# Five affine passes over the first token chunk move from the second projections' weight splits to the first output projection

## The chip, the core and the metric

The kernel runs on one core of one Trainium2 chip. A core has five instruction streams that run side by side and meet at semaphores: PE (TensorE, matrix products), DVE (VectorE), ACT (ScalarE), POOL (GpSimd), and SP (SyncE), which here only issues DMAs. The metric is the device time of one launch in microseconds (us). The kernel before took 1267.05 us, the median of three runs (1266.28 to 1267.63).

## The reference, cut to what matters

One decoder layer over 1024 tokens of width 1024. The part that the change touches is the first LayerNorm's result, which is needed twice: transposed, as the input of the projections, and by rows, as the residual of the first output projection.

```python
x = layer_norm(x, emb_ln_g, emb_ln_b)                 # rows: x_hat * g + b
proj = x @ w_in[l]                                    # pool channels u, queries q, latent c, indexer iq/ik/iw
pooled = causal_multiscale_pool(u_pool)               # windows 2, 4, 8, 16: one group of 128 channels each
pool_out = einsum(pooled, pool_w) * pool_scale
o_lat = dsa_sparse_attention(q_lat, c, iq, ik, iw, rel_bias)   # indexer scores, top 256, softmax
mix = concatenate([pool_out, attn_out]) @ w_o[l]      # the output projection
x = layer_norm(ALPHA * x + mix, ln1_g[l], ln1_b[l])   # the residual uses the rows x
ff = square(relu(x @ w_up[l])) @ w_down[l]
x = layer_norm(ALPHA * x + ff, ln2_g[l], ln2_b[l])
```

## The kernel before, in words

**Chunks and stages.** The tokens go in two chunks of 512, each of four blocks of 128 rows. The order on PE is: projections of chunk 0, projections of chunk 1, attention of chunk 0, output projection of chunk 0, MLP of chunk 0, then attention, output projection and MLP of chunk 1. Each stream's order is written out by hand; nothing is scheduled by a tool.

**Weights.** Every weight matrix is cut into units of 128 x 1024 numbers (512 KB). A unit passes three streams. SP loads it into one of four buffers of a ring (`wring`, `load_unit`); the load of unit n waits until unit n-4 has been split. ACT rounds it to the high part (`hi`, L1226). POOL, for most units, subtracts the two to get the low part (`lo`, which calls `split_lo`, L417). PE then forms hi x hi, hi x lo and lo x hi (L1540 to L1542). The output projection of chunk 0 has eight units, named wo(nh, u): nh is the half of the output columns, u the quarter of the inner dimension. The four of nh = 1 go to buffers of their own (`wo_hi`, `wo_lo`); the other four share the two `whi`/`wlo` buffers with everything else.

**The rows of chunk 0.** The normalized rows without gain and bias are spilled to memory early, and come back into `rows` before chunk 1's projections end. `emb_gains` on POOL then makes two passes over each of the four blocks: times the gain (L786), plus the bias (L788): eight passes, written mult0, add0, ..., mult3, add3 below. Each add raises the semaphore `emb_rows`. It is a generator: whoever calls `next` gets one pass. The gains lie in `gains`; once all four blocks are done, SP loads the gain and bias of the next LayerNorm over them (`load_gains`, L448 and L449).

**Around the pooling.** In `products(1)` PE projects q0, q1, q2, u0, u1, u2, u3 and q3 of chunk 1, and forms the four small products po0 to po3 (L1626) among and behind them. DVE makes the pooled channels in `pooling` (L584 to L604), with more and more adds from window 2 to window 16; po3 waits for the last. Meanwhile POOL splits the weights of the units ahead. The attention of chunk 0 begins behind po3: POOL prepares the head masks (L778, first wait on po3), DVE adds them to the logits (L1005).

**The output projection of chunk 0.** PE, DVE and ACT all walk the same list, `projection_steps`: first nh = 0 by u and then by block b, then nh = 1 by block and then by u. After each of the first sixteen steps one indexer dot product of chunk 1 is slipped in: PE forms it (`dot`, L1604 and L1605), ACT takes its relu (`relu_dots`, L1292), DVE adds it to the scores (`add_score`, L931). With two buffers for each, dot n waits for relu n-2, and relu n for score n-2. ACT also rounds the weights to come at set steps of the list: wo(1,1) at step (0,2,1) ahead of relu 25, wo(1,2) at (0,2,3) ahead of relu 27, wo(1,3) at (0,3,1) ahead of relu 29, the first MLP unit at (0,3,3) ahead of relu 31. `add_residual` on DVE adds the rows at u = 3 and takes the statistics; POOL turns them into 1/std (`inverse_std`, L743 and L745) behind its splits of the first two MLP units.

Of the kernel before, what the change touches and what calls it, by code (L numbers as in the profile page):

```python
# [41 lines left out]
CB = CHUNK // P  # L42
# [93 lines left out]
def layer(nc, x, emb_ln_g, emb_ln_b, rel_bias, w_in, pool_w, pool_scale, kv_norm_g, w_uk, w_uv, w_o,  # L136
# [15 lines left out]
    with ExitStack() as ctx:  # L152
# [3 lines left out]
        def sem(name):  # L156
            return ctx.enter_context(nc.semaphore(name))
# [125 lines left out]
        rows_in = sem("rows_in")  # L283
# [18 lines left out]
        emb_rows = sem("emb_rows")  # L302
# [47 lines left out]
        units = []  # L350
# [6 lines left out]
        U = {name: n for n, name in enumerate(units)}  # L357
# [54 lines left out]
        def split_lo(eng, name, sem_lo, at=None):  # L412

            n = U[name]

            eng.wait_ge(hi_ready, n + 1 if at is None else at)
            eng.tensor_tensor(parts_of(name, lo_tile(name)), parts_of(name, wring[n % 4]),  # L417
                              parts_of(name, hi_tile(name)).bitcast(F32), ALU.subtract).then_inc(sem_lo, 1)
# [11 lines left out]
        def _(sp):  # L430
            def load_unit(name):
                n = U[name]
                slot = wring[n % 4]
                if n >= 4:

                    sp.wait_ge(*LO[units[n - 4]])
                if name[0] == "wo":
                    _, c, nh, u = name
                    sp.dma_start(k_pairs(slot), wod[:, 2 * u:2 * u + 2, nh * 512:nh * 512 + 512]).then_inc(ring_in[n % 4], 16)
                elif name[0] == "ik":  # L440

                    sp.dma_start(parts_of(name, slot), wind[:, :, COL_IK:COL_IK + KEYW]).then_inc(ring_in[n % 4], 16)
                else:
                    col = {"c": COL_C, "iq": COL_IQ, "q": COL_Q, "u": COL_U}[name[0]] + (P * name[2] if name[0] != "c" else 0)
                    sp.dma_start(k_columns(slot), wind[:, :, col:col + P]).then_inc(ring_in[n % 4], 16)

            def load_gains(g, b):
                sp.dma_start(gains[:, 0, :], g.to_broadcast([P, D])).then_inc(gains_in, 16)  # L448
                sp.dma_start(gains[:, 1, :], b.to_broadcast([P, D])).then_inc(gains_in, 16)  # L449

            def load_mlp(c):

                first = U[("mlp", c, 0)]
                sem_lo, lo_base = LO[("mlp", c, 0)]

                sp.wait_ge(*LO[units[first - 1]])
                for g in range(GROUPS):
                    for j in range(GUNITS):
                        load_mlp_unit(c, g, j)
                        if c == 1:  # L460
                            if (g, j) == (0, 6):

                                sp.wait_ge(x1_rows, 2 * CB)
                                load_gains(ln2_g, ln2_b)
                            if j == 8 and g:
                                store(g - 1)
                            continue
                        if (g, j) == (0, 8):

                            sp.wait_ge(proj_full, 2 * CB)  # L470
                            sp.wait_ge(relu_ready, 48)
                            sp.dma_start(emb_rows_g[:, 0, :], emb_ln_g.rearrange("(o d) -> o d", o=1).to_broadcast([P, D])).then_inc(emb_gain_in, 16)
                            sp.dma_start(emb_rows_g[:, 1, :], emb_ln_b.rearrange("(o d) -> o d", o=1).to_broadcast([P, D])).then_inc(emb_gain_in, 16)
                        if j == 8:
                            load_stage(g)
                        if j == 4 and g:
                            store_stage(g - 1)
                if c:
                    store(CB - 1)
                    return  # L480
                store_stage(CB - 1)
# [32 lines left out]
            def load_units(names):  # L514
                for name in names:
                    load_unit(name)
# [40 lines left out]
            for b in range(CB):  # L557
                sp.dma_start(rows[:, b, :], spilld[b]).then_inc(rows_in, 16)
            load_units(units[U[("iq", 1, 3)]:U[("wo", 0, 1, 0)]])
            sp.wait_ge(emb_rows, CB)  # L560
            load_gains(ln1_g, ln1_b)
            load_units(units[U[("wo", 0, 1, 0)]:U[("mlp", 0, 0)]])
            load_mlp(0)
            load_units(units[U[("wo", 1, 0, 0)]:U[("wo", 1, 1, 0)]])

# [57 lines left out]
        def projection_steps():  # L623

            return [(0, u, b) for u in range(4) for b in range(CB)] + [(1, u, b) for b in range(CB) for u in range(4)]
# [5 lines left out]
        def dots_after(c, nh, u, b):  # L631

            return [16 + 4 * u + b] if c == 0 and nh == 0 else []

        def rows_of(c):
            return score if c else rows
# [67 lines left out]
        def _(pool):  # L704
# [58 lines left out]
            def head_masks(c):  # L763


                pool.wait_ge(g_full, EV[("po", 1, 3)])
                for m in range(32 * c, 32 * c + 32):
                    i, h = divmod(m, HEADS)
                    length = (i + 1) * P
                    near = min(NEAR, length)  # L770
                    if h == 0 and i >= 2:
                        pool.wait_ge(mask_ready, i - 1)
                    if m >= 2:

                        pool.wait_ge(masked, m - 1)
                    if h < 2 and length > NEAR:
                        pool.tensor_copy(mask[:, m % 2, 0:length - NEAR], score[:, i % CB, 0:length - NEAR])
                    pool.tensor_tensor(mask[:, m % 2, length - near:length], score[:, i % CB, length - near:length],  # L778
                                       near_bias[:, h, NEAR - near:NEAR], ALU.add).then_inc(mask_full, 1)

            def emb_gains():

                pool.wait_ge(gains_in, 32)
                for b in range(CB):
                    pool.wait_ge(rows_in, 16 * (b + 1))
                    link(pool.tensor_tensor(rows[:, b, :], rows[:, b, :], gains[:, 0, :], ALU.mult))  # L786
                    yield b
                    pool.tensor_tensor(rows[:, b, :], rows[:, b, :], gains[:, 1, :], ALU.add).then_inc(emb_rows, 1)  # L788
                    yield b
# [17 lines left out]
            def lo(*names):  # L807
                for name in names:
                    split_lo(pool, name, lo_pool)
# [24 lines left out]
            gained = emb_gains()  # L834
            for name in units[U[("iq", 1, 3)] + 3:U[("wo", 0, 0, 2)]]:
                lo(name)
                next(gained)
            head_masks(0)
            lo(*units[U[("wo", 0, 0, 2)]:U[("mlp", 0, 0)]])
            lo(("mlp", 0, 0), ("mlp", 0, 1))  # L840
            inverse_std(LN1_0)

# [29 lines left out]
        def _(dve):  # L872
# [203 lines left out]
            def add_residual(c, l):  # L1076


                dve.wait_ge(rows_in, 16 * CB * (c + 1))
                dve.wait_ge(emb_rows, CB * (c + 1))  # L1080
                for nh, u, b in projection_steps():
                    n = 8 * c + 4 * nh + b
                    if u == 3:
                        dve.wait_ge(proj_full, n + 1)
                        piece = rows_of(c)[:, b, nh * 512:nh * 512 + 512]
                        nc.vector.scalar_tensor_tensor(out=piece, in0=piece, scalar=ALPHA, in1=bank(("proj", c, nh, b))[:, :],
                                                       op0=ALU.mult, op1=ALU.add).then_inc(wo_added, 1)
                        dve.wait_ge(wo_added, n + 1)
                        nc.vector.bn_stats(stats[:, b, 6 * nh:6 * nh + 6], piece).then_inc(bn_ready, 1)
                        if nh == 1:  # L1090
                            dve.wait_ge(bn_ready, n + 1)
                            nc.vector.bn_aggr(mean_var[:, 4 * l + b, :], stats[:, b, :]).then_inc(stats_ready, 1)
                            x1_norm(c, l, b)
                            if b == CB - 2:
                                x1_lo(dve, c, 0, range(3))
                    if c and (nh, u, b) == (0, 2, CB - 1):
                        for piece in range(4):
                            split_lo(dve, ("wo", 1, 1, piece), lo_dve)
                    if c and (nh, u, b) in ((0, 3, CB - 1), (1, 0, 0)):
                        split_lo(dve, ("mlp", 1, nh), lo_dve)  # L1100
                    for d in dots_after(c, nh, u, b):
                        add_score(d)
                x1_lo(dve, c, 0, [3])
                x1_lo(dve, c, 1, range(4))
# [759 lines left out]
```

## Time and profile before

| what | value |
|---|---|
| median of the runs | 1267.05 us |
| the profiled execution's own time | 1263.58 us |
| its span | 1261.8 us |
| PE, DVE, ACT, POOL busy | 96%, 66%, 44%, 41% |
| chain that ended last | PE 84%, DVE 6%, POOL 5%, ACT 2%, issue 2%, DMA 1% |
| mean granted TensorE clock | 0.992 |

The profile is of one execution. Its busy shares are averages over stages with different limits, so a stage is read by itself, in its own stretch of the span. The chain that ended last is followed back from the last instruction, and says which engine's work or wait each microsecond hangs on. A row of a timeline shows in brackets how long the engine sat idle ahead of it and who released it. The granted clock is 1.00 where TensorE ran at 2.4 GHz and 0.50 where it ran at 1.2 GHz.

### The profile page before, as it was taken

The page shows a single profiled execution, that of the slowest core. Times are in us where ns is not written, and L with a number is a line of the kernel's source. Part 1 is how long each engine was busy: PE and PEld are TensorE (multiplying, and loading weights), DVE is VectorE, ACT ScalarE, POOL GpSimd, SP SyncE. Part 2 cuts the span into 40 slices and gives each one's busy share as a digit, 9 for nine tenths or more (in the row PEclk, how much of TensorE's full clock was granted, in tenths as well). Part 3 has the DMA queues.
Part 4 walks back from the last instruction along what each step waited for, and adds up shares of the span by engine and source line. Part 5 has one row for each costly group of instructions (what it writes and reads, how often), then busy time and mean ns, then how long its engine had stood idle before and what let it go on. Part 6 is the DMA issues. An engine that isn't in the chain of part 4 may idle for free.

```text
span 1261.8 us, 16530 instructions
## 1 busy us (share of the span) xinstructions
PE 1208.7 (96%) x5761; PEld 979.6 (78%) x5761; DVE 833.4 (66%) x1201; ACT 557.7 (44%) x943; POOL 512.5 (41%) x370
## 2 busy tenths in 40 slices
PE   5999997989999999999999999989899999999997
PEld 3776785778788778788788789978788888888886
DVE  6388989557857888888988766647534233243357
ACT  4546542775165234244243366652342442433440
POOL 2235798424435676775865752202102102103002
PEclk9999999899999999999999999999999999999999
DMA  7723431101314333243242200024132333423331
GB/s 221 250 76 106 145 100 52 66 1 34 101 34 134 100 101 117 84 133 100 84 132 90 94 1 2 1 101 134 63 100 88 105 101 95 117 84 99 116 102 66
DMA packets 126564, 117.59 MB, mean 93 GB/s; under 512 B 5741, under 2 KB 99498, under 8 KB 126506
## 3 DMA queue, kind: packets, MB, share of 16 engines
q1 hardware_dynamic: 126506, 116.81, 30.4%
q8 instruction: 37, 0.61, 0.2%
q14 instruction: 21, 0.17, 0.0%
HBM read 106.29 MB, written 10.50 MB: 93 GB/s over the span
## 4 chain that ended last, share of the span: by engine, by line
PE 84%; DVE 6%; POOL 5%; ACT 2%; issue 2%; DMA 1%; POOLq 0%; DVEq 0%; ACTq 0%
PE g_bank L1540 16%; PE g_bank L1542 16%; PE g_bank L1541 16%; PE wide L1540 9%; PE wide L1542 9%; PE wide L1541 9%; PE g_bank L1500 4%; POOL wlo L417 2%; PE wide L1645 1%; DVE win L588 1%; PE wide L1604 1%; PE wide L1605 1%; PE g_bank L1692 1%; POOL rows L805 1%; POOL rstd L745 1%
## 5 line engine op out<-in xcount | busy, mean ns | idle before, releaser
L417 POOL TENSOR_TENSOR wlo<-wring,whi 128x1024 fp32r<-128x1024 f32 (+1 forms) x94 | 229.6, 2444 | 226.0 <-ACT whi L1413 121.7
L1540 PE MATMUL g_bank<-xhi,whi 128*128 128x512 f32 (+2 forms) x768 | 300.7, 392 | 4.8 <-DVE xlo L654 3.8
L1542 PE MATMUL g_bank<-xhi,wlo 128*128 128x512 f32 (+2 forms) x768 | 296.9, 387 | 0.0
L1541 PE MATMUL g_bank<-xlo,whi 128*128 128x512 f32 (+2 forms) x768 | 296.8, 386 | 0.0
L1413 ACT ACTIVATE whi<-wring 128x1024 fp32r<-128x1024 f32 x120 | 127.1, 1059 | 355.8 <-PE wide L1542 179.8
L417 DVE TENSOR_TENSOR wlo<-wring,whi 128x1024 fp32r<-128x1024 f32 (+1 forms) x66 | 84.4, 1279 | 197.6 <-ACT whi L1413 192.7
L1540 PE MATMUL wide<-whi,hhi 128*128 128x512 f32 x480 | 190.2, 396 | 0.7 <-POOL wlo L417 0.7
L1542 PE MATMUL wide<-whi,hlo 128*128 128x512 f32 x480 | 189.6, 395 | 0.0
L1541 PE MATMUL wide<-wlo,hhi 128*128 128x512 f32 x480 | 189.6, 395 | 0.0
L1540 PEld LDWEIGHTS g_bank<-xhi,whi 128*128 128x128 f32 (+1 forms) x768 | 143.8, 187 | 39.9 <-DVE xlo L654 4.3
L1541 PEld LDWEIGHTS g_bank<-xlo,whi 128*128 128x128 f32 (+1 forms) x768 | 143.9, 187 | 33.0 <-issue 1.8
L1542 PEld LDWEIGHTS g_bank<-xhi,wlo 128*128 128x128 f32 (+1 forms) x768 | 143.8, 187 | 33.0 <-issue 0.6
L989 DVE MAX8 top<-work 128x8 f32<-128x640 f32 (+3 forms) x128 | 131.6, 1028 | 18.7 <-DVE work L992 0.2
L743 POOL TENSOR_SCALAR rstd<-mean_var 128x1 f32<-128x1 f32 x24 | 9.1, 381 | 301.5 <-DVE mean_var L884 232.9
L992 DVE MATCH_REPLACE8 work<-top,work 128x640 f32<-128x640 f32 (+3 forms) x128 | 129.2, 1010 | 0.0
L1540 PEld LDWEIGHTS wide<-whi,hhi 128*128 128x128 f32 x480 | 90.0, 187 | 24.5 <-POOL wlo L417 2.9
L1542 PEld LDWEIGHTS wide<-whi,hlo 128*128 128x128 f32 x480 | 90.0, 187 | 22.1
L1541 PEld LDWEIGHTS wide<-wlo,hhi 128*128 128x128 f32 x480 | 90.0, 187 | 21.8
L1226 ACT ACTIVATE whi<-wring 128x1024 fp32r<-128x1024 f32 (+1 forms) x40 | 41.6, 1041 | 115.7 <-PE g_bank L1542 99.5
L1005 DVE CUSTOM_DVE_ANT_0 logit<-wide,mask 128x128 f32<-128x128 f32 (+7 forms) x64 | 48.4, 756 | 53.2 <-PE g_bank L1500 44.9
L778 POOL TENSOR_TENSOR mask<-score,near_bias 128x256 f32<-128x256 f32 (+1 forms) x64 | 44.7, 701 | 74.0 <-DVE neg_max L1005 69.3
L931 DVE SCALAR_TENSOR_TENSOR score<-relu_sb,idx_w,score 128x384 f32<-128x384 f32 (+5 forms) x42 | 56.6, 1369 | 19.3 <-ACT relu_sb L1292 18.0
(215 smaller groups left out, 1993.4 us busy)
## 6 DMA issues: line engine op xcount, KB each, us to landing
wring<-in_w_up SPq DMA_DIRECT2D x64, 512.0 KB, 4.0
wring<-in_w_down SPq DMA_DIRECT2D x64, 512.0 KB, 3.7
wring<-in_w_in SPq DMA_DIRECT2D x26, 512.0 KB, 3.9
wring<-in_w_o SPq DMA_DIRECT2D x16, 512.0 KB, 4.6
rows<-in_x SPq DMA_DIRECT2D x8, 512.0 KB, 5.0
normalized_rows<-rows SPq DMA_DIRECT2D x8, 512.0 KB, 6.9
rows<-normalized_rows SPq DMA_DIRECT2D x4, 512.0 KB, 5.2
emb_stage<-normalized_rows SPq DMA_DIRECT2D x4, 512.0 KB, 4.8
```

The lines of the kernel that those rows point to most:

```text
L417: eng.tensor_tensor(parts_of(name, lo_tile(name)), parts_of(name, wring[n % 4]), parts_of(name, hi_tile(name)).bitcast(F32), ALU.subtract) ...
L778: pool.tensor_tensor(mask[:, m % 2, length - near:length], score[:, i % CB, length - near:length], near_bias[:, h, NEAR - near:NEAR], ALU. ...
L931: nc.vector.scalar_tensor_tensor(out=s, in0=relu_sb[:, n % 2, 0:length], scalar=idx_w[:, i, h:h + 1], in1=s, op0=ALU.mult, op1=ALU.add)\
L989: nc.vector.max(top8[:, 0, :], w).then_inc(topk_steps, 1)
L992: nc.vector.match_replace(w, top8[:, 0, :], w, TAKEN).then_inc(topk_steps, 1)
L1005: nc.vector.tensor_tensor_reduce(logit[:, m % 2, 0:length], wide[m % 2][:, 0:length], mask[:, m % 2, 0:length], -1.0, -TAKEN, ALU.add, ALU ...
L1226: nc.scalar.activation(parts_of(name, hi_tile(name)), parts_of(name, wring[n % 4]), ACT.Copy).then_inc(hi_ready, 1)
L1413: nc.scalar.activation(whi[(R[("mlp", c, 0)] + j) % 2][:, :], wring[(first + j + 2) % 4][:, :], ACT.Copy)\
L1500: last = nc.tensor.transpose(ps[:, n * P:n * P + rows_in_part] if rows_in_part == P else ps[:, 0:rows_in_part], part, ident[0:rows_in_part ...
L1540: nc.tensor.matmul(out_ap, w_hi, m_hi, start=first, stop=False)
L1541: nc.tensor.matmul(out_ap, w_hi, m_lo, start=False, stop=False)
L1542: return nc.tensor.matmul(out_ap, w_lo, m_hi, start=False, stop=last)
```

## The change

Three of the eight passes (mult0, add0, mult1) stay beside the weight splits of chunk 1's projections. The other five are taken behind the head masks of chunk 0: two behind the split of wo(0,2), two behind that of wo(0,3), one behind that of wo(1,0). `add_residual` waits for each block's own rows instead of for all four ahead of the first step. SP loads wo(1,0) ahead of its wait for the four blocks, and the other three units of nh = 1 still behind it.

```diff
@@ SP
             load_units(units[U[("iq", 1, 3)]:U[("wo", 0, 1, 0)]])
+            load_units(units[U[("wo", 0, 1, 0)]:U[("wo", 0, 1, 1)]])
             sp.wait_ge(emb_rows, CB)
             load_gains(ln1_g, ln1_b)
-            load_units(units[U[("wo", 0, 1, 0)]:U[("mlp", 0, 0)]])
+            load_units(units[U[("wo", 0, 1, 1)]:U[("mlp", 0, 0)]])
             load_mlp(0)
@@ POOL
             gained = emb_gains()
             for name in units[U[("iq", 1, 3)] + 3:U[("wo", 0, 0, 2)]]:
                 lo(name)
-                next(gained)
+                if name[0] == "u" and name[2] < 2 or name[0] == "q" and name[2] == 2:
+                    next(gained)
             head_masks(0)
-            lo(*units[U[("wo", 0, 0, 2)]:U[("mlp", 0, 0)]])
+            for name in units[U[("wo", 0, 0, 2)]:U[("mlp", 0, 0)]]:
+                lo(name)
+                for _ in range(2):
+                    next(gained, None)
@@ DVE, add_residual
-                dve.wait_ge(rows_in, 16 * CB * (c + 1))
-                dve.wait_ge(emb_rows, CB * (c + 1))
                 for nh, u, b in projection_steps():
                     n = 8 * c + 4 * nh + b
                     if u == 3:
+                        dve.wait_ge(rows_in, 16 * CB * (c + 1))
+                        dve.wait_ge(emb_rows, CB * c + (b + 1 if c == 0 else CB))
                         dve.wait_ge(proj_full, n + 1)
```

POOL's stream beside the projections of chunk 1, in the kernel before, from the split of the unit u2 to the first head mask (`wlo` is the low part of a weight unit):

```order
L417 TENSOR_TENSOR wlo1<-wring1,whi1 128x1024 [waits hi_ready,pool_steps]
L788 TENSOR_TENSOR rows<-rows,gains 128x1024
L417 TENSOR_TENSOR wlo0<-wring2,whi0 128x1024 [waits hi_ready]
L786 TENSOR_TENSOR rows<-rows,gains 128x1024 [waits rows_in]
L417 TENSOR_TENSOR wlo1<-wring3,whi1 128x1024 [waits hi_ready,pool_steps]
L788 TENSOR_TENSOR rows<-rows,gains 128x1024
L417 TENSOR_TENSOR wlo0<-wring0,whi0 128x1024 [waits hi_ready]
L786 TENSOR_TENSOR rows<-rows,gains 128x1024 [waits rows_in]
L417 TENSOR_TENSOR wlo1<-wring1,whi1 128x1024 [waits hi_ready,pool_steps]
L788 TENSOR_TENSOR rows<-rows,gains 128x1024
L778 TENSOR_TENSOR mask_56<-score,near_bias 128x128 [waits g_full]
```

In the changed kernel the five splits stand there alone. The five passes stand behind the last head mask of chunk 0, among the splits for the output projection (in this kernel's line numbers, L787 is the gain, L789 the bias; `wo_lo00` to `wo_lo03` belong to wo(1,0) to wo(1,3)):

```order
L417 TENSOR_TENSOR wlo0<-wring2,whi0 128x1024 [waits hi_ready]
L789 TENSOR_TENSOR rows<-rows,gains 128x1024
L787 TENSOR_TENSOR rows<-rows,gains 128x1024 [waits rows_in]
L417 TENSOR_TENSOR wlo1<-wring3,whi1 128x1024 [waits hi_ready,pool_steps]
L789 TENSOR_TENSOR rows<-rows,gains 128x1024
L787 TENSOR_TENSOR rows<-rows,gains 128x1024 [waits rows_in]
L417 TENSOR_TENSOR wo_lo00_90<-wring0,wo_hi00_82 128x1024 [waits hi_ready,pool_steps]
L789 TENSOR_TENSOR rows<-rows,gains 128x1024
L417 TENSOR_TENSOR wo_lo01_91<-wring1,wo_hi01_83 128x1024 [waits hi_ready]
L417 TENSOR_TENSOR wo_lo02_92<-wring2,wo_hi02_84 128x1024 [waits hi_ready]
L417 TENSOR_TENSOR wo_lo03_93<-wring3,wo_hi03_85 128x1024 [waits hi_ready]
```

SP's stream around the wait for the four blocks, before and with the change:

```order
-L439 DMA wring<-in_w_o 128x2x512 [waits lo_pool] x4
+L439 DMA wring<-in_w_o 128x2x512 [waits lo_pool] x5
 L448 DMA gains<-in_ln_g 128x1024 [waits emb_rows]
 L449 DMA gains<-in_ln_b 128x1024
-L439 DMA wring<-in_w_o 128x2x512 [waits lo_pool] x4
+L439 DMA wring<-in_w_o 128x2x512 [waits lo_pool] x3
 L507 DMA wring<-in_w_up 128x8x128 [waits lo_pool] x8
```

The wait on `emb_rows` stands one unit later in the stream, and what it waits for now ends in the output projection.

## Rows read from the trace of the kernel before

**Rows 1.** Page, part 4: chain that ended last, shares by engine.

```profile
PE 84%; DVE 6%; POOL 5%; ACT 2%; issue 2%; DMA 1%; POOLq 0%; DVEq 0%; ACTq 0%
```

**Rows 2.** Timeline of PE, 204 to 224 us: start, duration, line, instruction, [idle before <- releaser].

```profile
206.23 1.12 PE L1626 MATMUL g_bank<-pooledT,poolw 128*128 128x512 f32 x2 [0.65 <-DVE pooledT L604]
213.61 1.12 PE L1626 MATMUL g_bank<-pooledT,poolw 128*128 128x512 f32 x2 [0.65 <-DVE pooledT L604]
221.84 2.07 PE L1626 MATMUL g_bank<-pooledT,poolw 128*128 128x512 f32 x2 [7.10 <-DVE pooledT L604]
```

**Rows 3.** Timeline of DVE, pooling of chunk 1.

```profile
206.29 0.71 DVE L588 TENSOR_TENSOR win<-uT 128x527 f32<-128x527 f32 x1
...
214.61 2.55 DVE L588 TENSOR_TENSOR win<-win 128x526 f32<-128x526 f32 x1
217.20 2.19 DVE L593 COPY win<-uT 128x2 f32<-128x2 f32 x1
...
220.16 0.17 DVE L593 COPY win<-uT 128x4 f32<-128x4 f32 x1
...
221.09 0.69 DVE L604 SCALAR_TENSOR_TENSOR pooledT<-win,uT 128x512 f32<-128x512 f32 x1
```

**Rows 4.** Timeline of POOL, same stretch.

```profile
206.81 2.45 POOL L417 TENSOR_TENSOR wlo<-wring,whi 128x1024 fp32r<-128x1024 f32 x1 [1.18 <-ACT whi L1226]
...
214.26 2.34 POOL L417 TENSOR_TENSOR wlo<-wring,whi 128x1024 fp32r<-128x1024 f32 x1 [2.18 <-ACT whi L1226]
216.56 2.80 POOL L788 TENSOR_TENSOR rows<-rows,gains 128x1024 f32<-128x1024 f32 x1
224.00 0.87 POOL L778 TENSOR_TENSOR mask<-score,near_bias 128x128 f32<-128x128 f32 x2 [4.64 <-PE g_bank L1626]
```

**Rows 5.** Timeline of ACT, pooling of chunk 1.

```profile
206.63 0.58 ACT L1193 ACTIVATE uT<-g_bank 128x512 f32<-128x512 f32 x1
...
213.06 1.06 ACT L1226 ACTIVATE whi<-wring 128x1024 fp32r<-128x1024 f32 x1 [4.98 <-PE g_bank L1542]
```

**Rows 6.** Stretch: us, busy PE, PEld, DVE, ACT, POOL, then granted clock, DMA share, GB/s.

```profile
222.00:226.00 4.00, 3.77 (x10) 2.42 (x11) 0.60 (x4) 1.57 (x5) 1.74 (x4) 0.50 0.97 357
```

**Rows 7.** Timeline of POOL, output projection of chunk 0.

```profile
290.67 2.40 POOL L417 TENSOR_TENSOR wlo<-wring,whi 128x1024 fp32r<-128x1024 f32 x1 [21.99 <-ACT whi L1226]
299.39 2.42 POOL L417 TENSOR_TENSOR wlo<-wring,whi 128x1024 fp32r<-128x1024 f32 x1 [6.32 <-ACT whi L1226]
301.77 9.43 POOL L417 TENSOR_TENSOR wo_lo<-wring,wo_hi 128x1024 fp32r<-128x1024 f32 x3
```

**Rows 8.** Timeline of SP, issues around the gains of the next LayerNorm.

```profile
219.38 0.34 SPq L448 DMA_DIRECT2D gains<-in_ln_g  x1
...
220.25 0.43 SPq L439 DMA_DIRECT2D wring<-in_w_o  x1
```

**Rows 9.** DMA issues, 219.5 to 220.45 us, then 301 to 303 us: last number us to landing.

```profile
wring<-in_w_o SPq DMA_DIRECT2D x1, 512.0 KB, 7.5
...
wring<-in_w_o SPq DMA_DIRECT2D x1, 512.0 KB, 3.7
```

**Rows 10.** Timeline of ACT, output projection of chunk 0.

```profile
301.82 1.05 ACT L1226 ACTIVATE wo_hi<-wring 128x1024 fp32r<-128x1024 f32 x1
303.32 0.81 ACT L1292 ACTIVATE relu_sb<-wide 128x768 f32<-128x768 f32 x1 [0.44 <-PE wide L1605]
...
312.85 1.05 ACT L1226 ACTIVATE wo_hi<-wring 128x1024 fp32r<-128x1024 f32 x1
```

**Rows 11.** Timeline of PE there: dot 27, start of nh = 1, its end.

```profile
306.73 0.40 PE L1604 MATMUL wide<-key_hi,iq 128*128 128x512 f32 x1
...
316.38 0.39 PE L1540 MATMUL g_bank<-wo_hi,pool_hi 128*128 128x512 f32 x1
...
339.73 2.56 PE L1508 MATMUL wide<-ident 128*128 128x128 f32 x22
```

**Rows 12.** Timeline of DVE, last residual add of chunk 0.

```profile
342.02 0.68 DVE L1086 SCALAR_TENSOR_TENSOR rows<-rows,g_bank 128x512 f32<-128x512 f32 x1
```

## The prediction, made before the changed kernel ran

> **What bounds the kernel now.** I read the chain that ended last first: 84% of it is PE [rows 1]. So a microsecond counts where PE stands still, or where PE's next work comes later; where POOL or DVE merely get busier it costs nothing. I then looked on PE's timeline for idle time near the change. There is one big gap: PE has done po2 and stands 7.10 us until DVE has the last pooled tensor, so po3 starts only at 221.84 [rows 2]. The attention of chunk 0 hangs on it: the first head mask starts at 224.00, having waited for po3 [rows 4]. In the output projection of chunk 0, PE goes without a gap from the first step to 340.1 (the filler that follows it starts at 339.73, and I take 0.4 us for the last product's end) [rows 11]; there ACT, POOL and SP are early enough by a margin, and the change spends that margin. Those are the two places to work out.
>
> **Place 1: the pooling of chunk 1.** Beside POOL's work DVE's instructions are stretched. One and the same add takes 0.71 us when POOL is idle (it starts at 206.29, POOL's next pass starts at 206.81 and ends late) and 2.55 us when a weight split runs from 214.26 to 216.60: DVE starts at 214.61 and ends at 217.16, which is the split's end plus 0.56. A copy of 2 columns takes 2.19 beside a pass over the rows, one of 4 columns takes 0.17 alone [rows 3, 4]. So whoever comes second waits for the whole of the other's instruction. The Trainium skill ("SBUF — State Buffer", Who interferes with whom) says this of VectorE instructions with two SBUF inputs against GpSimd: an exclusive lock, not a sharing of bandwidth. By that rule, the trace agrees, but it also speaks against the change, since the score adds in the output projection read two SBUF inputs too.
>
> With the passes gone, DVE's last group (window 16) goes as follows. u3 reaches DVE at 206.63 + 0.58 = 207.21 [rows 5]. The split at 206.81 ends at 209.26 [rows 4] and holds the first copy until then. Behind it stand 4 adds at 0.71, 4 small instructions at 0.16 and the last one at 0.69 [rows 3], with about 0.04 between them: 4.4 us. The pooled tensor is there at 213.6. No other POOL pass lies in the way: the next split follows ACT's rounding, which waits for q3. q3 ends 0.65 us earlier than before, since po1's wait of 0.65 goes [rows 2] (its group ends well ahead); ACT rounds at 213.06 - 0.65 = 212.4 for 1.06 us [rows 5], and POOL splits from 213.6 to 216.0. Hence po3 starts near 213.7 instead of 221.84, and the first head mask, now behind the split, at 216.05 instead of 224.00: **7.95 us** earlier. Late next is thus POOL's split, not DVE.
>
> The clock adds a little. In the gap it falls to 0.50 and is still 0.50 from 222 to 226 while PE works [rows 6]: po3's two parts take 2.07 us where po2's take 1.12 [rows 2]. [...] What stands on the path after 224.00 are short products between longer waits; I take 0.75 us, bounds 0 and 1.5 (half of the 3 us or so of work at the low level). Place 1 gives **-8.7 us**, between -7.5 and -9.5.
>
> **Place 2: the output projection of chunk 0.** I keep the times of before here, and subtract place 1 at the end. POOL's split of wo(0,2) is at 290.67 to 293.07, followed now by add1 and mult2, which just fit ahead of the next split (299.39): even at 3.14 us each (see below) they end at 299.35 [rows 7]. From 299.39 five instructions now stand in a row: the split of wo(0,3), add2, mult3, the split of wo(1,0), add3. Alone one takes 2.40; three of them beside busy DVE score adds took 9.43, 3.14 each [rows 7]. Low end 5 x 2.40 = 12.0, high end 5 x 3.14 = 15.7. DVE has score adds in its queue for about three of the five and then runs dry (below), so 3 x 3.14 + 2 x 2.40 = 14.2: add3 ends, and `emb_rows` reaches 4, at **313.6** (311.4 to 315.1).
>
> Only then does SP leave its wait. It issues the two gain loads and wo(1,1), wo(1,2), wo(1,3). In the trace the same sequence starts at 219.38, the first unit is issued at 220.25 [rows 8] and lands 7.5 us later [rows 9]: 8.4 us from the end of the wait. The same load with nothing ahead of it lands in 3.7 [rows 9]; with the 0.9 us of issuing that is the low end, 4.6. I take 8.4, since the queue is the same: wo(1,1) is there at **322.0** (316.0 to 324). The Trainium skill ("DMA: Bandwidth & Descriptors", Anatomy of one DMA) gives some 2.0 us plus the bytes at 436 GB/s: for three loads of 512 KB an estimate of 5.6 us, by which the time would be 2.8 us shorter than I forecast. The trace shows more for the same three, so the sum goes by it.
>
> wo(1,1) is wanted early. ACT rounds it at 301.82, ahead of relu 25 [rows 10]. Its stream is in order, so ACT now stands at this rounding for 322.0 - 301.8 = 20.2 us. Queued behind it: relus 25 to 31 and all later roundings. Dot 27 needs relu 25, so PE stops where it stood at 306.73 [rows 11]. DVE runs out of scores after number 24. Nothing else can use the time: the projection steps of u = 3 stand behind dot 27 on PE.
>
> After the load (t = 322.0): rounding and relu 25 end at t + 1.8, and PE resumes. From there relus alternate with score adds, which wait behind POOL's splits: score 25 ends at t + 4.5, relu 27 at t + 5.5, score 26 at t + 8.0, relu 28 at t + 8.75, and then ACT rounds wo(1,3). Before, that was 312.85 - 301.82 = 11.0 us behind the rounding of wo(1,1); now it is 8.75, because the backlog of scores is gone: 2.3 us come back. Lateness from there: 20.2 - 2.3 = 17.9.
> The same by PE: it resumes at 323.8 instead of 306.73, 17.1 late. After 17 us of idle its clock will be at 0.50 for some 5 us, as it was after 7 us [rows 6], worth 2 to 3 us: it begins nh = 1 at t + 14.3 = 336.3 instead of 316.38, 19.9 late. But PE had some 1.9 us to spare: it ended at 340.1 while DVE, going block by block through the norm, made its last residual add at 342.02 [rows 11, 12]. 19.9 - 1.9 = 18.0. Both ways give **+18.0 us**. With the low end of the load (316.0) it is +12.0; with the high end (324) and all of the clock's price, +22.
>
> **The rest at nothing.** The per-block waits on DVE: block b's rows are ready at or ahead of 313.6, and the first step that wants them now comes past 323, so they never end last; behind such a wait would stand score adds. Without this edit DVE would have stood ahead of its first score. Loading wo(1,0) one place earlier only fills a free buffer. The next LayerNorm's gains land by 319, and are first used behind the statistics, past 340. From the MLP on all moves as one, since PE is the chain.
>
> **Sum.** 18.0 - 8.7 = **+9.3 us**. Against the profiled execution's 1263.58 that is 1272.9; the median of the runs stands 3.5 above it, and I apply the difference to the median: 1267.05 + 9.3 = **1276.4 us**.
>
> **Rivals.**
> A. A shorter stall. POOL's five instructions hardly meet DVE and the three units come in without a tail: t = 316.0, so +12.0 - 8.7 = +3.3, 1270.4. For it: a load alone lands in 3.7. Against: two 512 KB loads stand ahead of it in the same queue.
> B. A longer one. t = 324, and PE's low clock is not absorbed by the 1.9 us: +22 - 7.5 = +14.5, 1281.5. For it: no idle of 17 us is in the trace to show the recovery; against: the margin at 342.02.
> C. DVE's pooling is slow by itself, and place 1 gives nothing: +18.0, 1285. The pair of 0.71 and 2.55 us for the same instruction speaks against it.
> D. The faster side. The wait for wo(1,1) is not last: if its load came so early that place 2 costs less than 8.7 us, the kernel gains; with place 2 at nothing it takes 1267.05 - 8.7 = 1258.4. It decides from a landing at t = 312.7 in before's times. But five instructions of 2.40 us from 299.39 end at 311.4 and the load takes 4.6 at least, so it would need POOL to reach add3 earlier, or ACT to have slack of 3 us and more that I overlook.
>
> **Chances.** Forecast 0.60, A 0.17, B 0.13, C 0.04, D 0.06. A measurement of this kernel tells 0.2% (2.5 us) from no change. Slower by more: forecast, B, C and nearly all of A: 0.93. Within it: 0.03, the low edge of A. Faster: 0.04 of D. The range takes in A and most of B: 1270 to 1282.
>
> **What would show it.** Right: PE's wait ahead of po3 under 1.5 us and no low clock there; the first head mask near 216; on SP a wait for the rows' bias pass (L789) that ends in the output projection; on ACT 15 to 20 us idle ahead of a `wo_hi` rounding, put down to a DMA; PE idle some 16 us ahead of dot 27, the granted clock at 0.50 behind it. Wrong: ACT not idle there (D), the pooling's instructions still above 2 us with no split beside them (C), or `emb_rows` complete ahead of 311 in before's times. Then step "313.6" or step "8.4 us" has failed, and their rows say which.

## The result, and the profile after

The changed kernel took 1275.23 us (median of four runs, 1274.52 to 1278.06); the kernel before took 1266.91 us beside it. The ratio is 1.0070, 95% interval 1.0052 to 1.0087: about 8.3 us slower. The forecast was 9.3 us slower, 1276.4 us.

Both places are in the trace. First the pooling. This is PE's timeline of the changed kernel, 200 to 232 us; it answers to [rows 2]:

```profile
215.59 1.12 PE L1631 MATMUL g_bank<-pooledT,poolw 128*128 128x512 f32 x2 [0.69 <-DVE pooledT L605]
```

Of the three waits for pooled tensors one is left, the one ahead of po3, and it is 0.69 us instead of 7.10. DVE's timeline of the last channel group says why, beside [rows 3]:

```profile
209.26 2.00 DVE L585 COPY uT<-hist 128x16 f32<-128x16 f32 x1 [1.13 <-ACT uT L1198]
211.29 0.71 DVE L589 TENSOR_TENSOR win<-uT 128x527 f32<-128x527 f32 x1
212.03 0.15 DVE L594 COPY win<-uT 128x1 f32<-128x1 f32 x1
212.22 0.71 DVE L589 TENSOR_TENSOR win<-win 128x526 f32<-128x526 f32 x1
...
214.84 0.69 DVE L605 SCALAR_TENSOR_TENSOR pooledT<-win,uT 128x512 f32<-128x512 f32 x1
```

The add over 526 columns, 2.55 us before, takes 0.71. Only the first copy is held. POOL's timeline has the weight split that holds it, and behind the next split the first head mask (compare [rows 4]):

```profile
208.82 2.40 POOL L417 TENSOR_TENSOR wlo<-wring,whi 128x1024 fp32r<-128x1024 f32 x1 [4.06 <-ACT whi L1231]
215.27 2.47 POOL L417 TENSOR_TENSOR wlo<-wring,whi 128x1024 fp32r<-128x1024 f32 x1 [4.05 <-ACT whi L1231]
217.70 0.86 POOL L779 TENSOR_TENSOR mask<-score,near_bias 128x128 f32<-128x128 f32 x2
```

Clock times of two profiled executions must not be subtracted as they stand. This one is 2.0 us late when the pooling begins, a point that the change doesn't reach (DVE's first copy starts at 191.60, before at 189.59); its first projections ran partly at the lower clock (granted clock 0.91 from 20 to 40 us, 1.00 in before). So I measure from that copy. The first mask came 34.41 us behind it before, and 26.10 us now: 8.3 us are won.

Now the output projection. These are POOL's seven instructions from the split of wo(0,3) on, as in [rows 7]:

```profile
293.39 2.44 POOL L417 TENSOR_TENSOR wlo<-wring,whi 128x1024 fp32r<-128x1024 f32 x1 [0.64 <-ACT whi L1231]
295.79 3.26 POOL L789 TENSOR_TENSOR rows<-rows,gains 128x1024 f32<-128x1024 f32 x1
299.01 3.33 POOL L787 TENSOR_TENSOR rows<-rows,gains 128x1024 f32<-128x1024 f32 x1
302.42 2.81 POOL L417 TENSOR_TENSOR wo_lo<-wring,wo_hi 128x1024 fp32r<-128x1024 f32 x1
305.19 2.33 POOL L789 TENSOR_TENSOR rows<-rows,gains 128x1024 f32<-128x1024 f32 x1
315.56 5.43 POOL L417 TENSOR_TENSOR wo_lo<-wring,wo_hi 128x1024 fp32r<-128x1024 f32 x2 [8.04 <-ACT wo_hi L1231]
```

add3 ends at 307.52. SP's timeline has the issue of the gains at that moment:

```profile
307.55 0.34 SPq L448 DMA_DIRECT2D gains<-in_ln_g  x1
```

And this is ACT's timeline, with the same rounding as the first of [rows 10]:

```profile
314.43 1.06 ACT L1231 ACTIVATE wo_hi<-wring 128x1024 fp32r<-128x1024 f32 x1 [16.85 <-DMA wring<-in_w_o]
```

ACT stood 16.85 us for one load. PE waits for the relu behind it, ahead of dot 27, and works at the lower clock afterwards. Its row and the stretches (columns as in [rows 6]), beside [rows 11]:

```profile
316.24 0.79 PE L1609 MATMUL wide<-key_hi,iq 128*128 128x512 f32 x1 [15.43 <-ACT relu_sb L1297]
```

```profile
304.00:316.00 12.00, 0.00 (x0) 0.00 (x0) 0.00 (x0) 1.57 (x2) 3.96 (x3) 0.54 0.61 216
316.00:320.00 4.00, 3.76 (x9) 2.99 (x10) 3.78 (x2) 2.96 (x4) 3.92 (x2) 0.50 0.04 14
320.00:322.00 2.00, 2.00 (x8) 1.61 (x7) 2.00 (x2) 0.00 (x0) 0.99 (x1) 0.50 0.00 0
322.00:330.00 8.00, 8.00 (x37) 6.63 (x37) 7.90 (x9) 3.39 (x4) 2.41 (x1) 0.99 0.28 78
```

The last residual add of chunk 0 answers to [rows 12]:

```profile
352.08 0.69 DVE L1091 SCALAR_TENSOR_TENSOR rows<-rows,g_bank 128x512 f32<-128x512 f32 x1
```

From DVE's first pooling copy to this add it is 352.08 - 191.60 = 160.48 us; before it was 342.02 - 189.59 = 152.43. The difference, 8.05 us, is close to that of the medians, 8.3. This distance is the ruler for all runs below, since it leaves out the scatter at either end. It is still one execution of each kernel: where that execution lies far from the median of its runs, I say so.

### The profile page after: what moved, and what is told of

It is laid out like the page before. It is cut to its first block, busy times and chain, and to the rows that moved or that the text cites. A ratio compares the mean times of both kernels' runs of the same rounds, so it can differ in the third digit from the quotient of the medians.

```text
span 1273.7 us, 16544 instructions
## 1 busy us (share of the span) xinstructions
PE 1212.2 (95%) x5761; PEld 983.0 (77%) x5761; DVE 828.8 (65%) x1201; ACT 557.3 (44%) x943; POOL 512.0 (40%) x370
## 4 chain that ended last, share of the span: by engine, by line
PE 80%; POOL 8%; DVE 4%; ACT 3%; DMA 2%; issue 2%; SPq 0%; POOLq 0%; DVEq 0%; ACTq 0%
PE g_bank L1545 16%; PE g_bank L1547 15%; PE g_bank L1546 15%; PE wide L1545 8%; PE wide L1547 8%; PE wide L1546 8%; PE g_bank L1505 3%; POOL wlo L417 3%; POOL rows L806 2%; PE wide L1650 1%; DMA wring<-in_w_o 1%; PE wide L1609 1%; PE wide L1610 1%; PE g_bank L1697 1%; POOL rstd L746 1%
## 5 line engine op out<-in xcount | busy, mean ns | idle before, releaser
L994 DVE MAX8 top<-work 128x8 f32<-128x640 f32 (+3 forms) x128 | 131.6, 1028 | 18.7 <-DVE work L997 0.2
L936 DVE SCALAR_TENSOR_TENSOR score<-relu_sb,idx_w,score 128x384 f32<-128x384 f32 (+5 forms) x42 | 64.0, 1549 | 27.8 <-ACT relu_sb L1297 26.6
```

The source lines that it names most:

```text
L936: nc.vector.scalar_tensor_tensor(out=s, in0=relu_sb[:, n % 2, 0:length], scalar=idx_w[:, i, h:h + 1], in1=s, op0=ALU.mult, op1=ALU.add)\
L994: nc.vector.max(top8[:, 0, :], w).then_inc(topk_steps, 1)
```

## The experiments

My theory: two effects that add up. Without the passes beside it the pooling is 8 us shorter; SP's wait for all four blocks, moved into the output projection, makes wo(1,1) late, which costs 16 to 18. The rivals were that the passes' own work is what costs there (P), and rival C of the prediction.

| kernel | median, us | ratio to before (95%) | first mask behind first copy | last residual add behind it |
|---|---|---|---|---|
| before | 1266.3 to 1267.1 | 1 | 34.41 | 152.43 |
| changed | 1275.23 | 1.0070 (1.0052 to 1.0087) | 26.10 | 160.48 |
| passes left out | 1259.52 | 0.9951 (0.9933 to 0.9968) | 26.10 | 144.40 |
| late load alone | 1272.64 | 1.0055 (1.0037 to 1.0073) | 34.40 | 160.00 |
| units loaded first | 1266.98 | 1.0005 (0.9995 to 1.0016) | 26.09 | 152.51 |
| gains loaded last | 1272.54 | 1.0055 (1.0039 to 1.0071) | 26.09 | 157.60 |
| one wait for all blocks | 1275.67 | 1.0079 (1.0063 to 1.0096) | 26.10 | 160.56 |
| five behind the masks | 1263.57 | 0.9980 (0.9970 to 0.9990) | 26.09 | 147.97 |
| five and three | 1262.29 | 0.9967 (0.9955 to 0.9978) | 27.82 | 148.28 |
| four and four | 1260.05 | 0.9954 (0.9941 to 0.9966) | 26.10 | 146.99 |

Each ratio is to runs of the kernel before on the same chip. The last two columns are from the one profiled execution of each.

**Passes left out: place 1 alone.**

```diff
+            pool.wait_ge(pool_steps, steps[0])
+            pool.sem_inc(emb_rows, CB - 1)
             head_masks(0)
...
                 lo(name)
-                for _ in range(2):
-                    next(gained, None)
```

> The changed kernel without the five moved passes: blocks 1 (bias), 2 and 3 of chunk 0 are added as a residual without gain and bias (that part of the computation is left out), and SP is released as soon as the third pass is done. It measures place 1, the pooling of chunk 1, by itself. My theory (DVE's pooling instructions wait for POOL's passes): the first head mask as early as in the changed kernel, no wait for a late load in the output projection, 8 us below the kernel before: 1259 us (1257.5 to 1260). Rival C (the pooling is slow by itself, place 1 gives nothing): 1267. If both places interact, the sum of this one's gain and the next one's loss will not give the changed kernel's +8.3.

It took 1259.52 us, ratio 0.9951: 6.2 us (4.1 to 8.5) below the kernel before by the ratio, and 8.03 us by the ruler. The first mask comes exactly as in the changed kernel. Rival C falls: place 1 is worth its 8 us in the traces, and the interval of the ratio holds that value.

**Late load alone: place 2 without the passes.** In the kernel before:

```diff
+            load_units(units[U[("wo", 0, 1, 0)]:U[("wo", 0, 1, 1)]])
             sp.wait_ge(emb_rows, CB)
+            sp.wait_ge(*LO[("wo", 0, 1, 0)])
             load_gains(ln1_g, ln1_b)
-            load_units(units[U[("wo", 0, 1, 0)]:U[("mlp", 0, 0)]])
+            load_units(units[U[("wo", 0, 1, 1)]:U[("mlp", 0, 0)]])
```

> The kernel before with SP's stream alone changed: wo(1,0) is loaded ahead of the gains, and the gains and the other three units wait until POOL has split wo(1,0) (about 304.1 us in the times of before). All eight passes stay beside chunk 1's projections, so POOL and DVE do just what they did. My theory (the late load of wo(1,1) holds ACT, and ACT holds PE through relu 25): lands at 304.1 + 6.9 = 311.0, ACT stands 9 us, 2.5 of it come back, so 6.5 us above the kernel before: 1273.5 us (1272 to 1275). Rival (the passes' own time on POOL, and what they do to DVE, are what costs in the output projection, not the load): 1267.

It took 1272.64 us, ratio 1.0055. POOL and DVE have the same work as before and the kernel is still 7 us slower, so a late load costs time without any help from the passes. ACT's timeline:

```profile
313.73 1.06 ACT L1228 ACTIVATE wo_hi<-wring 128x1024 fp32r<-128x1024 f32 x1 [10.53 <-DMA wring<-in_w_o]
```

PE waited 7.38 us ahead of dot 27 here, and by the ruler the stage is 7.6 us longer.

```profile
315.54 0.80 PE L1606 MATMUL wide<-key_hi,iq 128*128 128x512 f32 x1 [7.38 <-ACT relu_sb L1294]
```

**Units loaded first: the passes without the late load.** In the changed kernel:

```diff
-            load_units(units[U[("wo", 0, 1, 0)]:U[("wo", 0, 1, 1)]])
+            load_units(units[U[("wo", 0, 1, 0)]:U[("mlp", 0, 0)]])
             sp.wait_ge(emb_rows, CB)
             load_gains(ln1_g, ln1_b)
-            load_units(units[U[("wo", 0, 1, 1)]:U[("mlp", 0, 0)]])
```

> The changed kernel with all four units of nh = 1 loaded ahead of SP's wait, as a buffer comes free; the gains follow the wait. The five passes stay among the splits. If the late load were all of place 2's price, the kernel would keep place 1's gain: 1259. My theory says that once the load is early the passes themselves come last: the splits of wo(1,1) to wo(1,3) now stand behind add3, end near 324.5 instead of 316.4 in the times of before, and the load of the first MLP unit and with it the norm of block 0 move by as much: about +8 - 8 = 0, 1267 us (1264.5 to 1269).

1266.98 us, ratio 1.0005, the interval around 1. Repairing the load gives back 8 us, not 16, as forecast: behind the load stands POOL's queue. Its timeline has the three splits behind add3 and then the first MLP units' splits:

```profile
304.68 3.08 POOL L788 TENSOR_TENSOR rows<-rows,gains 128x1024 f32<-128x1024 f32 x1
307.71 9.52 POOL L417 TENSOR_TENSOR wo_lo<-wring,wo_hi 128x1024 fp32r<-128x1024 f32 x3
322.68 5.75 POOL L417 TENSOR_TENSOR wlo<-wring,whi 128x1024 fp32r<-128x1024 f32 x2 [5.45 <-ACT whi L1230]
```

SP issues the first MLP unit's load as the third of those splits ends (317.23; in before 316.38, with the issue at 316.41), and ACT stands until it has landed:

```profile
317.26 11.57 SPq L507 DMA_DIRECT2D wring<-in_w_up  x6
```

```profile
321.54 1.06 ACT L1230 ACTIVATE whi<-wring 128x1024 fp32r<-128x1024 f32 x1 [5.56 <-DMA wring<-in_w_up]
```

Behind the first pooling copy this rounding comes at 130.52 us, against 123.04 in the kernel with the passes left out (313.50 - 190.46): 7.5 of the 8.1 us by the ruler. So P is true as well, at half the size, but hidden in the changed kernel: while ACT waits for the load, POOL has time for the passes. The two costs of place 2 do not add; the later one counts.

**Gains loaded last.**

```diff
-            load_gains(ln1_g, ln1_b)
             load_units(units[U[("wo", 0, 1, 1)]:U[("mlp", 0, 0)]])
+            load_gains(ln1_g, ln1_b)
```

> The changed kernel with SP's two gain loads behind wo(1,1) to wo(1,3) instead of ahead of them, all four blocks still waited for. In the changed kernel ACT's rounding of wo(1,1) starts 6.9 us after add3's end. Theory (the load's lateness passes to PE one for one, and two loads ahead of it cost their share of the queue): wo(1,1) alone needs 0.1 + 3.7 us, so 3.1 us come back: 1272 us (1271 to 1273.5). Rival (the landing is a fixed delay and loads side by side cost nothing, or the first MLP unit's load behind them is the limit): 1275, as the changed kernel.

1272.54 us, 2.7 us below the changed kernel by the medians (1.9 by the ratios, whose intervals overlap) and 2.9 us by the ruler. ACT's wait fell from 16.85 to 13.77:

```profile
310.23 1.06 ACT L1231 ACTIVATE wo_hi<-wring 128x1024 fp32r<-128x1024 f32 x1 [13.77 <-DMA wring<-in_w_o]
```

ACT started 3.8 us behind add3's end (306.39) instead of 6.9. Here 3.1 us of landing were 2.9 us of the kernel, and the two loads ahead in the queue cost 3.

**One wait for all blocks.**

```diff
-                        dve.wait_ge(emb_rows, CB * c + (b + 1 if c == 0 else CB))
+                        dve.wait_ge(emb_rows, CB * c + CB)
```

> The changed kernel with DVE's first residual add waiting for all four blocks instead of one each. I priced the per-block form at nothing against this one, since the first residual add comes some 15 us behind add3: 1275 us (1274 to 1276.5), as the changed kernel. Rival (the per-block waits save DVE time at the first steps of u = 3): 2 us or more above it, 1277.

1275.67 us against 1275.23, with intervals of the ratios that overlap, and 160.56 against 160.48 by the ruler: nothing, as priced.

**Five behind the masks.** Where the trace of before has POOL idle, 21.99 us ahead of the split of wo(0,2) [rows 7]:

```diff
             head_masks(0)
-            for name in units[U[("wo", 0, 0, 2)]:U[("mlp", 0, 0)]]:
-                lo(name)
-                for _ in range(2):
-                    next(gained, None)
+            for _ in gained:
+                pass
+            lo(*units[U[("wo", 0, 0, 2)]:U[("mlp", 0, 0)]])
```

> The changed kernel with the five passes right behind the last head mask of chunk 0, ahead of the split of wo(0,2), where POOL stood idle for 22 us (268.7 to 290.7 in the times of before). They need 12.0 to 15.7 us, so no split is late; the gains and wo(1,1) are in before 292, 10 us ahead of ACT. Left is what DVE loses at the end of the attention, where it splits the mixed rows and scales the last heads beside those passes: 0 to 2.5 us. My theory: 8 - 1 = 7 us below the kernel before, 1260 us (1258.5 to 1262). Rival (DVE's waits behind the passes at the end of the attention cost as much as they did in the pooling): 1265 or more.

1263.57 us: faster than before (0.9980, 0.9970 to 0.9990), but 3.6 us short of my 1260, outside my range. By the ruler 3.6 of the 8 us are lost. The loads came in time. Lost was time at the end of the attention, more than I had allowed. First DVE's split of the pooled rows, then PE waiting for the head scaling behind it:

```profile
268.40 5.50 DVE L1064 TENSOR_TENSOR pool_lo<-pool_out,pool_hi 128x512 fp32r<-128x512 f32 x4 [0.30 <-ACT pool_hi L1367]
```

```profile
274.79 1.11 PE L1504 MATMUL g_bank<-ident,att 128*128 128x128 f32 x4 [3.73 <-DVE att L1045]
```

Four instructions that took 2.50 us take 5.50, beside the last two passes; PE's idle time is 3.73 us (1.16 before, so 2.6 more), and the clock falls:

```profile
272.00:274.00 2.00, 0.00 (x0) 0.00 (x0) 2.00 (x4) 0.00 (x0) 0.14 (x1) 0.50 0.42 131
274.00:276.00 2.00, 1.22 (x5) 1.22 (x6) 0.69 (x2) 0.06 (x1) 0.00 (x0) 0.50 0.97 295
276.00:278.00 2.00, 2.00 (x6) 1.52 (x6) 0.71 (x2) 1.91 (x4) 0.00 (x0) 0.50 0.93 344
278.00:280.00 2.00, 2.00 (x10) 1.62 (x9) 1.78 (x3) 1.41 (x3) 0.00 (x0) 0.80 0.07 25
```

In the same stage of before it stayed at 1.00. The rest, 1 us, fits the six products that now start every 0.43 us instead of every 0.23 there: 1.2 us as an estimate.

**Five and three, then four and four.** Fewer passes behind the masks, more in the pooling:

```diff
-                if name[0] == "u" and name[2] < 2 or name[0] == "q" and name[2] == 2:
+                if name[0] == "u" or name[0] == "q" and name[2] == 2:
```

with the rest of the eight behind the masks as above; the second kernel has `name[2] < 3` in place of `< 2`.

> Passes placed by what the runs showed: five beside the splits of q2, u0, u1, u2 and u3 (mult0, add0, mult1, add1, mult2), three right behind the last head mask (add2, mult3, add3). The two more in the pooling fall where DVE waits for its next channel group anyway (it stood idle 2.07 and 1.21 us there in the changed kernel); the three end 7.2 us behind the last mask, before DVE splits the mixed rows (8.5 us behind it). So place 1's gain stays and neither the att scaling nor the load of wo(1,1) is late: 8 us below the kernel before, 1258.5 us (1257 to 1260.5). Rival (every pass beside the pooling lengthens it by its own 2.4 us, up to po3): 1261 to 1263.

1262.29 us, outside my range too. My rival had the number, but not the mechanism: it let every pass cost its own 2.4 us, and the next kernel shows that the fourth pass costs nothing at the first mask. DVE's timeline:

```profile
208.39 2.92 DVE L605 SCALAR_TENSOR_TENSOR pooledT<-win,uT 128x512 f32<-128x512 f32 x1
...
214.98 2.72 DVE L605 SCALAR_TENSOR_TENSOR pooledT<-win,uT 128x512 f32<-128x512 f32 x1
```

The fifth pass made the third channel group so late that its last instruction ran into the next split, and the fourth group's into the one after that. The first mask came 1.7 us later. Another 2.4 us were lost up to the split of wo(0,2), although DVE's split of the pooled rows took 2.50 us as before; the granted clock was 0.64 from 276 to 280 us of this execution, and what the clock and what the passes took there is not separated. This execution took 1263.88 us, 1.6 above the median, and its mean granted clock, 0.988, is the lowest of the nine, which go up to 0.994: the low clock may not come in each of them.

> As the five-and-three kernel, but mult2 goes from behind the split of u3 to behind the last head mask: four passes beside the splits of q2, u0, u1, u2 and four behind the last mask. In the five-and-three kernel mult2 pushed DVE's third channel group into the next split (its last instruction took 2.92 us), and the fourth group's last instruction into the split after that (2.72 us for 0.69), so that the first head mask waited 1.81 us for po3. Theory: with mult2 gone from there po3 and the first mask come as in the changed kernel, and four passes behind the last mask end 9.6 us later, 1 us into DVE's split of the pooled rows, which leaves 0 to 1 us of loss: 7 to 8 us below the kernel before, 1259 us (1257.5 to 1260.5). Rival (DVE's loss there is the same as with five passes, +2.6 us and the low clock behind it): 1262.5 or more.

1260.05 us, ratio 0.9954 (0.9941 to 0.9966), inside my range. With the interval it can't be told from the kernel with the passes left out (0.9951). DVE's split of the pooled rows costs 1.0 us:

```profile
271.04 3.49 DVE L1064 TENSOR_TENSOR pool_lo<-pool_out,pool_hi 128x512 fp32r<-128x512 f32 x4 [0.30 <-ACT pool_hi L1367]
```

In the profiled execution more than that is lost. By the ruler it is 146.99 - 144.40 = 2.6 us behind the kernel with the passes left out: PE waited 1.73 us ahead of the transposes instead of 1.16, and the granted clock was 0.75 from 274 to 276 us and 0.50 from 276 to 278. This execution took 1261.54 us, 1.5 above the median of the six, and that of the kernel with the passes left out 1258.37, 1.2 below its own. Of place 1's 8 us the ruler gives 5.4 as kept, the ratio 5.8 (4.3 to 7.5). This version is faster than both kernels.

## Why the prediction was right, point by point

**Place 1, -8.7 us forecast.** Measured 8.3 at the first mask, where the forecast without the clock had 7.95. The sum stood at 4.4 us for the last channel group behind the split's end; it was 215.53 - 211.22 = 4.3. What is late next was POOL's split of wo(0,1), as forecast: the first mask follows it without idle time. The clock's 0.75 us did not come, and no run shows that term. PE waited only 0.69 us ahead of po3 and the clock was 1.00 there, but PE stood 1.53 us once more, for DVE's first logits (until 218.69), which the sum had not priced, and the granted clock was 0.50 from 220 to 223 us. 8.1 us of the 8.3 are left at ACT's rounding of wo(0,2) (91.86 against 99.94 us behind the first copy). So the 8.7 came near by luck in part: the mask was 0.35 us better than forecast, and the way from there 0.9 worse. Rival C is refuted by the kernel without the passes.

**add3's end, 313.6 forecast.** In before's times (by that rounding, 283.46 against 289.53, so 6.07 more) it ended at 307.52 + 6.07 = 313.59. The passes took 3.26 and 3.33 us while DVE had score adds queued, the last one 2.33 us once DVE had run dry.

**The landing, 8.4 us forecast.** This was the term mis-sized: 6.9 us from add3's end to ACT's start. The trace of before had 7.5 us for the third load of such a queue, the new one 6.0, although three loads followed the gains here and two there. The low end, with nothing ahead, was 4.6. The rule of the Trainium skill ("DMA: Bandwidth & Descriptors", Anatomy of one DMA) had given 5.6 us as an estimate. That section states its fit for DMAs that GpSimd issues, and these come from SP, so it was a loose one. The measured 6.9 lies between it and the 8.4 from my row. A single load's landing in one execution was too thin a base for a term that goes in one for one.

**What comes back, 2.3 us forecast.** From the rounding of wo(1,1) to that of wo(1,3) it was 322.80 - 314.43 = 8.37 us (8.75 forecast, 11.03 before): 2.7 back. Lateness 314.43 + 6.07 - 301.82 = 18.7, less 2.7 is 16.0; measured from rounding of wo(0,2) to the last residual add it is 16.1 (68.62 against 52.49 us).

**The clock there.** PE idle 15.4 us, then 0.50 until about 322. From dot 27 to nh = 1 PE took 328.66 - 316.24 = 12.4 us (12.5 forecast, 9.65 before). So the low clock and the relus' spacing together cost PE 2.8 us, and PE entered nh = 1 some 18.3 us late against 16.1 at the last residual add: PE's margin there took the difference, as argued. That the margin is what absorbs it was not tried by a run of its own.

**The sum.** 16.1 - 8.1 = +8.0 by the traces, +8.3 by the medians, +9.3 forecast. Place 2 was forecast 1.9 us too dear (1.5 of it the landing, 0.4 what comes back) and place 1 0.6 too good; the two misses partly cancel, which is luck.

**The step at nothing.** The per-block wait, confirmed. Not foreseen: that the passes' own lateness on POOL would have cost 8 us without the late load. I had priced the load alone, and the kernel with the units loaded first shows what stood right behind it.

## What to carry to other kernels

When work moves to another place in a stream, look for every wait that hangs on its last piece, and what is queued behind each: here one SP wait for a semaphore carried two gain loads and three weight loads with it. Of an engine's idle time, ask what the others do in it: in these traces a POOL pass cost up to 2 us where DVE had a short instruction with a waiting consumer, and nothing where DVE had time to make it up (the fourth pass in the pooling), so the gap to fill is one in which both POOL and the path are idle. Two late things at one place don't add up; repairing the later one uncovers the other.

## What the runs showed of the hardware

A 2-column copy on DVE took 2.19 us beside a POOL pass and 0.17 alone, and in the changed kernel a 16-column copy took 2.00 us. Each ended within 0.04 us of the POOL instruction beside it (219.39 and 219.36, 211.26 and 211.22): what these held instructions cost is the rest of the other's, whatever their own size. The reverse was milder: a POOL pass of 2.33 us grew to 3.26 and 3.33 beside DVE's score adds.

At the end of the attention the clock fell in three of these kernels, and no single length of idle time goes with it. At 272 us with five passes behind the masks it fell beside a wait of 3.73 us. With five and three it was 0.64 from 276 to 280 us although PE's wait ahead of the transposes there was 1.16 us, as in before, where it stayed at 1.00. PE's busy time in the five stretches of 2 us up to that point is the same in both (1.30, 1.87, 1.38, 1.25, 1.02 us from 268 to 278 us; 1.30, 1.87, 1.37, 1.25, 1.02 from 272 to 282 in before). What does differ there is the DMA queue: SP's loads moved 339 and 282 GB/s from 274 to 278 us with five and three, and nothing in before. Loads are not needed for a fall, though: in the changed kernel the clock fell at 220 us with none running, and with five passes behind the masks it stood at 0.50 by 272.00, before SP issued its loads at 272.17. No run separates the loads from chance. What decides it in this stage stays open. The price of such waits can therefore be more than their length, and I would not put a number on it from another kernel's trace.
